# Rows of a token ordered by expert: lower-expert rows gathered before the last expert tile is stored, and added by VectorE

## The reference

```python
def hier_moe(h, w_group, b_group, w_exp, b_exp, w_gate, w_up, w_down):
    """Top-1 expert group, then top-2 experts inside it; gated-MLP experts."""
    ...
    e_w = jax.nn.softmax(e_val, axis=-1) * g_w
    expert_id = g_idx * EXPERTS_PER_GROUP + e_idx
    combine = jnp.sum(jax.nn.one_hot(expert_id, N_EXPERTS, dtype=jnp.float32) * e_w[..., None], axis=1)
    hid = jax.nn.silu(jnp.einsum('nd,edf->nef', xt, w_gate)) * jnp.einsum('nd,edf->nef', xt, w_up)
    hid = hid * combine[:, :, None].astype(hid.dtype)
    out = jnp.einsum('nef,efd->nd', hid, w_down)
```

## Time and profile before

| | |
|---|---|
| median of 3 runs | 1293.52 us (1293.06 to 1294.37) |
| span of the profiled execution | 1292.1 us |
| TensorE busy (PE) | 1231.2 us, 95% |
| VectorE busy (DVE) | 582.2 us, 45% |
| ScalarE busy (ACT) | 414.0 us, 32% |
| GpSimd busy (POOL) | 57.9 us, 4% |
| mean granted TensorE clock over the span | 0.991 |
| shares of the chain that ended last | PE 81%, DMA 4%, DVE 4%, ACT 3% |

### The profile page before, as it was taken

The page is one execution under the profiler, slowest core; times in us unless marked ns, Lnnn a source line. Parts: engine busy times, 40 slices in busy tenths (PEclk is TensorE's granted clock), DMA queues, the critical chain, the costliest instruction groups (busy, mean ns, idle before and its releaser), DMA issues.

```text
span 1292.1 us, 17212 instructions
## 1 busy us (share of the span) xinstructions
PE 1231.2 (95%) x5561; PEld 681.7 (53%) x5562; DVE 582.2 (45%) x1310; ACT 414.0 (32%) x859; POOL 57.9 (4%) x63
## 2 busy tenths in 40 slices
PE   7999999999999999998978998899999999999997
PEld 4554566666664475443435444466654574444442
DVE  1322555555552574322217444888834663222215
ACT  2432444444451120111113326677722111111122
POOL 0103000000000020000011000000000110000002
PEclk9999999999999999999999999999999999999998
DMA  9979999622253067999976001500020369989946
GB/s 373 413 310 407 415 412 411 256 100 99 99 204 147 33 231 241 353 356 358 368 281 266 9 1 36 229 2 1 1 98 2 123 259 347 351 268 352 358 169 242
DMA packets 88357, 290.18 MB, mean 225 GB/s; under 512 B 9209, under 2 KB 27580, under 8 KB 86876
## 3 DMA queue, kind: packets, MB, share of 16 engines
q1 hardware_dynamic: 46032, 185.68, 39.1%
q0 software_dynamic: 16640, 64.59, 12.7%
q10 hardware_dynamic: 25612, 38.96, 8.9%
HBM read 214.48 MB, written 74.73 MB: 224 GB/s over the span
## 4 chain that ended last, share of the span: by engine, by line
PE 81%; DMA 4%; DVE 4%; ACT 3%; SPq 3%; issue 2%; ACTq 1%; DVEq 0%; POOL 0%; POOLq 0%
PE ps L2099 16%; PE ps L1709 11%; PE ps L1726 11%; PE ps L2128 8%; PE ps L1651 7%; PE ps L1979 6%; PE ps L1942 4%; PE ps L1754 3%; PE ps L1803 3%; PE ps L2178 3%; PE ps L1671 2%; DMA arena<-in_moe_gu 2%; PE ps L1935 2%; PE ps L1952 2%; PE ps L2041 2%
## 5 line engine op out<-in xcount | busy, mean ns | idle before, releaser
L2099 PE MATMUL ps<-arena 128*128 (+1 forms) x560 | 247.9, 596 | 0.0
L2099 PEld LDWEIGHTS ps<-arena 128*128 128x128 f32 x560 | 104.4, 191 | 118.4 <-issue 118.3
L1651 PE MATMUL ps<-const,arena 128*128 128x128 f32 (+2 forms) x1000 | 144.0, 277 | 18.3 <-DMA const<-in_const 8.4
L1709 PE MATMUL ps<-arena 128*128 128x512 f32 (+2 forms) x400 | 152.1, 535 | 5.0 <-DVE arena L1111 1.8
L1651 PEld LDWEIGHTS ps<-const,arena 128*128 128x128 f32 (+2 forms) x1000 | 114.7, 141 | 76.9 <-issue 39.6
L1149 DVE TENSOR_REDUCE hst<-ps 128x1 f32<-128x640 f32 (+1 forms) x160 | 110.8, 713 | 94.3 <-PE ps L1979 80.1
L1726 PE MATMUL ps<-arena 128*128 128x512 f32 x320 | 142.0, 596 | 1.4 <-issue 1.4
L2128 PE MATMUL ps<-arena 128*128 (+1 forms) x280 | 126.1, 593 | 2.2 <-ACT arena L850 2.2
L727 ACT ACTIVATE arena<-ps,hst 128x640 f32<-128x640 f32 (+1 forms) x160 | 112.4, 706 | 42.0 <-DVE hst L1149 42.0
L1709 PEld LDWEIGHTS ps<-arena 128*128 128x128 f32 x400 | 74.4, 190 | 74.4 <-issue 58.3
L1726 PEld LDWEIGHTS ps<-arena 128*128 128x128 f32 x320 | 59.1, 190 | 69.8 <-issue 69.7
(11 more groups left out here) (213 smaller groups left out, 1212.2 us busy)
## 6 DMA issues: line engine op xcount, KB each, us to landing
arena<-in_moe_gu SPq DMA_DIRECT2D x128, 512.0 KB, 12.7
arena<-in_ada_w SPq DMA_DIRECT2D x62, 768.0 KB, 11.8
slot_rows<-arena POOLq DMA_DIRECT2D x10, 4096.0 KB, 68.1
arena<-in_moe_w_down SPq DMA_DIRECT2D x64, 512.0 KB, 15.8
slot_rows<-arena ACTq DMA_DIRECT2D x33, 512.0 KB, 8.7
arena<-slot_rows ACTq DMA_DIRECT2D x124, 128.0 KB, 13.1
arena<-mod_rows SPq DMA_DIRECT2D x12, 512.0 KB, 12.6
arena<-in_gqa_w_qkv SPq DMA_DIRECT2D x12, 512.0 KB, 14.8
```

Source lines behind the costliest of these rows:

```text
L1651: return nc.tensor.transpose(out, in_, ident[0:rows, 0:rows])
L1709: last = mm(bank(2 + b, cols), hT[l](t)[:, k * P:(k + 1) * P], w[:, k], start=k == 0, stop=k == KD - 1)
L2099: last = mm(bank(gu_bank(u)), e_xsT[:, nth(u, D)][:, k * P:(k + 1) * P], w(k * BANK, BANK), start=k == 0, stop=k == KD - 1)
```

## The change

The two rows of a token are now ordered by their place in `slot_rows`, that is by expert. `place_rows` writes the smaller row number first and the larger second; `order_weights`, new, exchanges the two weights of a token where its rows were exchanged. The rows of the lower expert ("low") can't lie in the last expert tile, so their five gathers wait only for the stores of all tiles but the last: `k` = 0 (`fourth_stored`), 1 and 2 (`early_stored`). The five gathers of the higher expert's rows ("high") wait for `last_stored`, now the two halves of the last tile, and for the low gather of their tile.

VectorE adds the low rows to `X` by itself (`add_low`: a multiplication by weight and gate, then an addition). In layer 0 it does so for tiles 0 to 3, then `combine(0)`, and tile 4 after `mod_cols(1, 0)`. In layer 1 it does so for all five tiles before the first gating, and TensorE adds only `X` and the gated high rows. `combine` now has two operations, and ScalarE's `scale` is gone. `turn_tables` and `order_weights` stand inside the last expert tiles. TensorE's first `keep_busy` and SP's loads of pieces 1 and 2 wait for both gathers of tile 0.

```diff
-    e_g = [ar(2 * D * b, 2 * D) for b in range(4)] + [ring(SLOT + HALF_SLOT, 2 * D)]
+    e_low = [ar(t * D, D) for t in range(NTILE)]
+    e_high = [ar(NTILE * D + t * D, D) for t in range(3)] + [ring(SLOT + HALF_SLOT + t * D, D) for t in range(2)]
...
+    def gathered(l, t, high):
+
+        return S(f"gathered{t}"), 32 * l + 16 * high + 16
...
-            if b == 1:
-                sp.wait_ge(gathered(0, 0), gathers(0, 0))
             if b < 2:
                 end = end_of(NE - RING_N + b)
                 sp.wait_ge(S("gu_done", 0), end)
-            else:
-                sp.wait_ge(gathered(0, 1), gathers(0, 0))
+            if b:
+                sp.wait_ge(*gathered(0, 0, 1))
             in_pieces(landed(name), slot_of(name), A["gqa_w_qkv"][b])
...
-            pool.wait_ge(S("last_stored"), 16 * (RING_N + 1) * (l + 1))
+            pool.wait_ge(S("fourth_stored"), 16 * (l + 1))
+            pool.wait_ge(S("early_stored"), 32 * (l + 1))
             for t in range(NTILE):
-                for c in range(2):
-                    pool.indirect_dma_start(
-                        e_g[t][:, c * D:(c + 1) * D], None, slots,
-                        bass.IndirectOffsetOnAxis(ap=slot_i[:, 2 * t + c:2 * t + c + 1], axis=0))\
-                        .then_inc(gathered(t, c), 16)
+                pool.indirect_dma_start(e_low[t], None, slots, bass.IndirectOffsetOnAxis(ap=slot_i[:, 2 * t:2 * t + 1], axis=0))\
+                    .then_inc(S(f"gathered{t}"), 16)
+            pool.wait_ge(S("last_stored"), 32 * (l + 1))
+            for t in range(NTILE):
+                pool.wait_ge(*gathered(l, t, 0))
+                pool.indirect_dma_start(e_high[t], None, slots, bass.IndirectOffsetOnAxis(ap=slot_i[:, 2 * t + 1:2 * t + 2], axis=0))\
+                    .then_inc(S(f"gathered{t}"), 16)
...
-        scale(0, 1)
         late_columns(1)
-        scale(0, 2)
         square_g(1)
...
-            op(nc.vector.tensor_copy(slot_i[:, 2 * t:2 * t + 2], pl)).then_inc(S("slotted"), 1)
+            settle()
+            nc.vector.tensor_tensor(slot_i[:, 2 * t:2 * t + 1], pl[:, 0:1], pl[:, 1:2], ALU.min)
+            nc.vector.tensor_tensor(slot_i[:, 2 * t + 1:2 * t + 2], pl[:, 0:1], pl[:, 1:2], ALU.max).then_inc(S("slotted"), 1)
...
+        def order_weights():
+
+            rows = split(rt(R_PL, 2 * NTILE), NTILE)
+            first, second = w_pair[:, 0:NTILE], w_pair[:, NTILE:]
+            turned, a, b = (rt(R_FREE + k * NTILE, NTILE) for k in range(3))
+            op(nc.vector.tensor_tensor(turned, rows[:, :, 0], rows[:, :, 1], ALU.is_gt))
+            op(nc.vector.tensor_tensor(a, second, turned, ALU.mult))
+            nc.vector.tensor_tensor(b, first, turned, ALU.mult)
+            op(nc.vector.tensor_tensor(second, second, a, ALU.subtract))
+            nc.vector.tensor_tensor(first, first, b, ALU.subtract)
+            op(nc.vector.tensor_tensor(second, second, b, ALU.add))
+            nc.vector.tensor_tensor(first, first, a, ALU.add)
...
+                if k == 0:
+                    order_weights()
+                if l == 0 and k == 1:
+                    turn_tables()
...
+        def gated(rows, t, c):
+
+            return nc.vector.scalar_tensor_tensor(rows, rows, w_pair[:, c * NTILE + t:c * NTILE + t + 1], gate_row(t), ALU.mult, ALU.mult)
+
+        def add_low(l, t):
+
+            if t == 0:
+                dve.wait_ge(S("gates_m"), 32 * (l + 1))
+            dve.wait_ge(*gathered(l, t, 0))
+            gated(e_low[t], t, 0)
+            settle()
+            last = nc.vector.tensor_tensor(xt(t), xt(t), e_low[t], ALU.add)
+            if l:
+                last.then_inc(S("low_added"), 1)
+            settle()
 
         def combine(t):
 
+            dve.wait_ge(*gathered(0, t, 1))
+            gated(e_high[t], t, 1)
             settle()
+            nc.vector.tensor_tensor(xt(t), xt(t), e_high[t], ALU.add).then_inc(S("combined", 0), 1)
+
+        def gate_high(t):
+
+            dve.wait_ge(*gathered(1, t, 1))
+            gated(e_high[t], t, 1).then_inc(S("gated"), 1)
...
         experts(0)
-        turn_tables()
-        combine_first()
+        for t in range(LAT):
+            add_low(0, t)
+        combine(0)
         row_stats("mix1", 0, 1)
         norm(1, 0)
         mod_cols(1, 0)
+        add_low(0, LAT)
         combine(1)
         row_stats("mix1", 1, 2)
         norm(1, 1)
...
         experts(1)
-        gate_chosen(0)
-        gate_chosen(1)
+        for t in range(NTILE):
+            add_low(1, t)
+        gate_high(0)
+        gate_high(1)
...
             if l:
-                pe.wait_ge(gathered(0, 1), gathers(0, 0))
+                pe.wait_ge(*gathered(0, 0, 1))
                 keep_busy(10, 2)
                 pe.wait_ge(S("combined", 0), 1)
                 keep_busy(4, 2)
...
             for t in range(LAT):
                 if t == LAT - 1:
-                    pe.wait_ge(S("last_stored"), 16 * (RING_N + 1) * 2)
+                    pe.wait_ge(S("last_stored"), 32 * 2)
+                pe.wait_ge(S("low_added"), t + 1)
                 part(t, xt(t), True)
             for t in range(NTILE):
-                for c in range(2):
-                    pe.wait_ge(S("gated"), 2 * t + c + 1)
-                    last = part(t, e_g[t][:, c * D:(c + 1) * D], False, c == 1)
-                last.then_inc(S("combined", 1), 1)
+                pe.wait_ge(S("gated"), t + 1)
+                part(t, e_high[t], False, True).then_inc(S("combined", 1), 1)
```

54 lines of the change are left out of this document (10 added, 44 removed).

## The result

The changed kernel took 1304.54 us in the median of 4 runs (1300.06 to 1306.21), the kernel before 1293.94 in 4 runs on the same chip: a ratio of 1.0076, with a 95% interval of 1.0064 to 1.0088. It is slower, by some 10 us where 3 were forecast. The profiled execution has a span of 1303.0 us in place of 1292.1, so 10.9 us are to be found.

The account below looks back on a forecast made before the run. TensorE is busy 95% of the span, so a change pays only where it stands still, at the end of either layer's experts. + 4.0 - 0.6 + 1.2 + 0.2 - 1.6 = + 3.2 on 1293.52 gives 1296.7 us, range 1292.5 to 1300.5.

Parts of the forecast that it names:

- The five pairs: Layer 0, VectorE: five gate-and-add pairs of 2.66 us, 13.3 in all, before `combined` of tile 0, which comes 4.0 us later.
- The lead of the early gathers: Both layers: low gathers wait for an earlier store, so the first starts 4.0 us sooner (4.04 in layer 1).
- TensorE's clock: Layer 0's end: keep-busy matmuls with more holes may lose clock; 0 to 2.8 us, 1.2 taken.
- ScalarE's scale: Layer 0, ahead of `project`: without the scale `late_columns` starts sooner; gain 0.6 us.
- The ordering: `place_rows`: one more tiny operation per layer in VectorE's chain before `feed_first`; + 0.2 us in all.
- High rows of tile 0: Layer 0: sixth in the gather queue, expected in time with 0.3 us to spare; rival that they come late, 1298.0, chance 0.10.
- Layer 1: Kernel's end: earlier gathers, five more adds on VectorE, which ends last, and half TensorE's sums after the gatings; - 1.6 us.
- a wait between the low adds: Sign of being wrong: VectorE waiting for gathers between the low adds, where none was expected.
- POOL beside a busy VectorE: Gather issue beside dense adds might slow, up to 2.3 us on the sum under the skill's lock; 0 taken.
- the change does not do what it says: Rival: low gathers go out only with the last store, both starts 4 us later; 1304.7 us, chance 0.02.
- Clock lost at both ends: Rival: TensorE's clock falls in layer 0 and in layer 1; + 6.5, 1300.0 us, chance 0.13.
- Early adds are free: Rival: VectorE's low adds fall wholly under waits for gathers; - 4.1, 1289.4 us, chance 0.10.

Follow-up runs that it names:

- e1: Changed kernel, but in layer 0 VectorE adds each tile's low rows just ahead of that tile's `combine`; 1297.74 us, ratio 1.0029.
- e4: Changed kernel with more keep-busy matmuls at layer 0's end, starting at the landing of tile 0's low rows; 1300.51 us, ratio 1.0053.
- e2: e1 with tile 0's high rows gathered second in layer 0, ahead of the other tiles' low rows; 1296.91 us, ratio 1.0019.
- e11: e7 with layer 0's gathers in the old order by tiles, ScalarE's `scale` and the three-operation combination for tiles 1 to 4 back; 1291.15 us, ratio 0.9980.
- e9: Kernel before plus only the ordering of a token's two rows, with `order_weights` and `turn_tables` in the last expert tiles; 1292.81 us, ratio 0.9989.
- e7: Layer 0 of e5, layer 1 of e3, SP's weight pieces at one gather of tile 0 each, longer keep-busy; 1293.29 us, ratio 0.9988.
- e10: e7 with layer 1's low gathers also waiting for the last store, so no gather is early; 1296.30 us, ratio 1.0013.
- e3: Changed kernel, but in layer 1 VectorE only gates the low rows and TensorE adds them in PSUM; 1300.91 us, ratio 1.0039.
- e5: e2 with tile 0's low rows in layer 0 also waiting for the last store; 1296.36 us, ratio 1.0008.

## Why the prediction failed

**Direction and mechanism.** "Slower", by VectorE's order in layer 0, held: e1 undoes that order and gains 5.2 us in layer 0, the clock's share included. The size did not: 3.2 us were forecast, 10.9 came in the span, and the time lies above the range.

**Layer 0: +4.6 forecast (4.0 - 0.6 + 1.2), +7.6 measured.** The five pairs took 13.39 us, as forecast (13.3), and without a wait. Three terms were mis-sized, by 1.2 + 1.3 + 0.4 us.
- *The lead of the early gathers*: 4.0 us taken, 2.8 measured (VectorE starts 8.31 us behind D0 in place of 11.10). The store did land 4.0 us sooner. 0.5 us went between landing and first issue (0.79 and 0.26 us), and 0.6 in the first gather's landing (4.94 us from issue to VectorE, 4.34 before). Cost 1.2.
- *TensorE's clock*: 1.2 taken, 2.5 measured (e4). The upper end of my bounds, 2.8, was nearer. I took a value under the middle because both rows were "as near". They weren't, and not for the length of the hole, which e1 has too without the loss. The keep-busy matmuls were broken in two and ended at 689.92, TensorE stood for 1.80 us ahead of the turns (0.31 before, none in e1), and the clock, which was up, fell again. That the break did it is read from the rows; no run changed it alone. Cost 1.3. The Trainium skill's sentence that I set beside it (TensorE: Matmul & The Clock Gate, Part 1: The HAM clock gate) pointed the right way.
- *The norm*: 0.46 us of issue ahead of it, 0.09 before, not in the sum. e4 has it too, e1 and e2 don't, e11 has it ahead of another norm; its cause is open. Cost 0.4.

*ScalarE's scale*: 0.6 taken, and right: from VectorE's modulated columns to `project` it is 1.60 us, 2.21 before. But e9 keeps the scale and has 1.64, because tile 1's first rows landed sooner and the scale ran 19.16 us behind D0, not 19.69: the term hangs on a landing. *The ordering*: + 0.2 taken; e9 shows no cost. High rows of tile 0 were in time; that rival didn't matter while VectorE was later still. It did matter in e1, where they cost 5.62 us of VectorE's time.

**Layer 1: -1.6 forecast, +2.4 measured.** This step failed most. VectorE's additions end 22.9 us behind D1, where the sum had 20.7: 0.9 of lead missing, and 1.33 us of waiting for the second low rows, which landed 7.6 us after their issue; a wait between the low adds is one of the signs of being wrong that the prediction names. I had said no wait, from an average over all ten gathers; the first two follow one another more slowly. In layer 1 of the kernel after and of e7 VectorE's first two low rows start 3.9 and 4.0 us apart, in e10, where the gathers come behind the stores, 2.5, and before 1.7. Then TensorE's sum for tile 0 took 2.7 us to ScalarE's start, not 1.8, its second half at half clock; and the rest of the tail, 11.1 us from the first `final` on, 0.8 more than forecast. 0.9 + 1.3 + 0.9 + 0.8 is 3.9 of the 4.0 us. (In the other profiles with this layer 1 the miss is 2.5 to 3.7.) The deeper fault is that the working followed VectorE and checked TensorE only behind the gatings. The earlier trace rows show TensorE's sums of `X` at work beside the gathers; made to wait for `low_added`, they became a 7.3 us hole with a lower clock behind it (0.50 from 1271). e3 takes that away together with VectorE's five additions: -5.0 us.

**Store and early gathers.** The working let the last store land as before, 2.0 us, and found the high gathers held by POOL's queue alone. e2 and e7 show it at 4.3 to 4.4 us beside early gathers, the changed kernel at 4.5. There it does not hold the high gathers up: POOL goes from the fifth gather to the sixth without waiting for it. It is why e2 can't gain. The Trainium skill says that DMAs issued from SP, ACT and GpSimd run on the same 16 DMA engines (DMA: Bandwidth & Descriptors, Issuing engines are not separate DMA queues) and that each engine takes its queues in turn, packet by packet (DMA: Bandwidth & Descriptors, Queues, rings and completion order). The runs agree in sign: the store from ScalarE's queue lands later while POOL's gather is under way. The 2.4 us that the store lands later could not have been had from it.

**POOL beside a busy VectorE.** I weighed a lock between the two, which the Trainium skill states (SBUF — State Buffer, SBUF: two separate sides) for a VectorE operation with two SBUF inputs and a GpSimd operation that reads SBUF. The trace has one gather per layer that fits it, and at the size of one operation at most. In layer 0 the gather issued 0.10 us after VectorE had begun its first two-input operation took 1.99 us in place of 0.94, those beside the dense work that followed 1.00 to 1.22. In layer 1 one issued 0.23 us after the second such operation took 1.86, but the one issued 0.05 us after the first took 0.94.

```profile
675.42 1.99 POOL L651 DMA_INDIRECT arena<-slot_rows,slot_i  x1 [0.30 <-DMA arena<-slot_rows,slot_i]
677.72 1.00 POOL L656 DMA_INDIRECT arena<-slot_rows,slot_i  x1 [0.30 <-issue]
679.02 1.22 POOL L656 DMA_INDIRECT arena<-slot_rows,slot_i  x1 [0.30 <-issue]
```

If every gather issued beside such an operation waited for it, all of these would be long; one is. The long one came ahead of tile 0's high rows, which were still in time: it cost the changed kernel nothing.

**The rivals.** The nearest number is that of "the change does not do what it says" (1304.7), and it is luck: its mechanism is out, since the low gathers did go out ahead of the last store. "Clock lost at both ends" (1300.0) was the nearest in mechanism, with 2.5 of its 2.8 us in layer 0 and some 0.9 of its 1.7 in layer 1; with the lead (1.2 and 0.9) and the wait in layer 1 (1.3) added it comes to 1303.4. "Early adds are free" is out: the pairs lay one behind another. (Its price was also worked out at landings 1.6 us apart, where its own condition, over 2.66, does not hold.) The range failed because the cases moved one term each, while lead, clock, norm and wait all erred on the same side.

**What stays open.** The 0.79 us between store and gather: e9 has 0.26 like the kernel before, and every kernel with POOL's new list of waits 0.79 ahead of its first gather, e5 too, where no gather goes before the last store. In e2 the second gather, which waits for the last store by itself, follows it by 0.26. I tried nothing that tells the waits themselves from the new destinations. The norm's 0.46 us, the 1.0 us at the span's end and the rest of the first and fifth columns are open as well.

## What to carry to other kernels

Work that is made early is worth its lead only if nothing more urgent stands behind it: put what the waiting engine needs first (tile 0's two row blocks), on VectorE and in the gather queue alike, and the rest behind it, tile by tile. Before an addition is moved from one engine to another, look at what the relieved engine did with it: here TensorE's sums were useful work under a wait, and with them back in e3 its clock stayed up. And an early DMA is not free for the store that runs beside it; price that store again.

## What the hardware showed

- Two half stores of 256 KB from ScalarE's queue land in 2.0 us each alone, and in 2.0 to 2.2 and 4.3 to 4.5 with an indirect gather of 512 KB or several under way (after, e2, e7; back to 2.0 in e10).
- In layer 1 the early gathers were worth 3.8 us (e7 against e10), 1.7 us of it as clock, in layer 0 one early gather 0.6 (e2 against e5). My reading, not tested: what counts is how much of the following work can use rows that come early.
- TensorE's granted clock in layer 0: after a hole of 12.9 us and 5.8 us of small matmuls it was up (0.96 from 690 to 692), and behind a stand of 1.80 us it was 0.50 again from 692 to 698. The turns' way to the modulation took 1.9 us in place of 1.1, `project`'s first 32 records 15.66 in place of 13.97. In e1, with a hole of 12.79 us and no stand ahead of the turns, they took 13.97.
- Stands of TensorE of 2.27 us (before, layer 1) and 2.49 us (e10, layer 1) were followed by 0.53 to 0.62; one of 2.41 us in e7 was not (1.00), one of 2.24 us at the same place in e10 was (0.50). So in these rows the length of a stand alone does not tell.
